# Splitting the tail of a decoder block into five stages, with the second token tile's layers ahead of the last two and the first expert dot products inside the first tile's queries

## The chip, the cores and the metric

The kernel runs on one core of a Trainium2 chip. The metric is the device time of one execution in microseconds; three runs of the kernel before gave 4187.27, 4188.42 and 4192.22 us, median 4188.42 us. Everything is in 32-bit floats.

## What is computed

One decoder block on 512 tokens of 2048 channels: a normalised and modulated input, a mixer (12 heads of windowed attention beside a convolution module, merged by two sigmoid gates and projected), a residual, a second norm, and a retrieval layer over 16384 single-neuron experts. Cut to what the change touches:

```python
y = (g_attn * attn + g_conv * conv) @ w_out        # "mix", then "out"
x = x + gate1 * rms_norm(y, g[1])
h = rms_norm(x, g[2]) * (1.0 + scale2) + shift2
q = (h @ w_q).reshape(B, S, 8, 2, 128)             # queries
s1, s2 = q[..., 0, :] @ sub_keys[:, 0], q[..., 1, :] @ sub_keys[:, 1]
v1, i1 = top_k(s1, 16); v2, i2 = top_k(s2, 16)
top, ci = top_k(v1[:, None] + v2[None, :], 16)     # 16 experts of each of 8 heads
gate = softmax(top)
pre = einsum('td,tkd->tk', h, expert_down[idx])    # 128 rows of 2048 for every token
out = einsum('tk,tkd->td', gelu(pre) * gate, expert_up[idx])
x = x + gate2 * rms_norm(out, g[3])
```

## The kernel before, in words

Each engine runs its own program and they meet at semaphores. The first part (to about 843 us) makes the projections, the attention and the convolution of all 512 tokens. What follows has two interleaved strands.

**The tail.** `TAIL` (L31) has two parts: tokens 0 to 127, then tokens 128 to 511. Each goes through the same steps, and each reads the weights again in chunks of 1 MB that SP loads into a ring of buffers (`T_KB`, L144: five buffers for the first part, three for the second; `put`, L489). One part is 48 chunks of the mix (four column groups `cg`, each of gate chunks `ga` x4, `gc` x4, attention projection `ao` x2 of half size, convolution projection `co` x2), 16 chunks of the output projection (`out`), one chunk of x per 128 tokens (`x`), and 16 chunks of the queries (`q`, four groups, each followed by the key scores `sc`). A chunk is 16 matmuls on TensorE of as many columns as the part has tokens. ScalarE applies the sigmoids and copies, VectorE the products, the norms, and then `route` (L1552, six steps that pick 16 experts for each of two heads) and `gates` (L1589, the end of the softmax, behind an exponential that ScalarE makes in `gate_exp`, L1127). POOL first loads 32 MB of modulation weights (L570 to L575, ring `ada_ring` of four), which VectorE sums in `condition` (L1516) while the first part's mix runs.

**The retrieval.** It goes in blocks: block b stands for 32 tokens times 4 of their 128 experts, so 512 blocks (`BLOCKS`), 128 for each tile of 128 tokens. POOL gathers 1 MB of expert rows for each block from the down table (L594) and, 22 blocks behind (`UP_LAG`), 1 MB from the up table (L602). Both gathers of one step of the loop stand in one queue, and each first waits until its buffer is free: a down buffer by VectorE's `dot` (L1602), an up buffer by TensorE's `weighted_rows` (L840), which runs 24 blocks behind (`LAG`). ScalarE makes the gelu and the block's weights (`unit_gelu`, `block_weights`); VectorE multiplies by the gates in `unit_act` once in 16 blocks. Once in 32 blocks TensorE turns the next rows of h (`h2_quarter`, with a copy by ScalarE after each quarter), and the 32 finished tokens are normalised and stored (`z_sum`, `x2_rows`, `finish`, `stores`).

**Their interleaving.** Each engine keeps a position in blocks, and `retrieve(upto)` brings it forward. In the second part of the tail each engine calls it after a chunk, or after some chunks (`chunk_out`, `passed`), with a block number from `PACE` (L121 to L126): block 128 at chunk 83, evenly. In the first part nothing of the retrieval runs. After the tail, `retrieve(END)` does the rest, 384 blocks. The gathers have three down and three up buffers up to block `WIDE` = 160, and five and five from there, some of which are the tail's memory, hence the waits at L592 and L600. SP loads the keys again for the second part once `routed` is 4 (L535).

## Time and profile before

| | us |
|---|---|
| median of three runs | 4188.42 |
| the profiled execution, device time | 4186.43 |
| its span, first to last instruction | 4184.6 |
| TensorE busy in the span | 2812.4 (67%) |
| VectorE busy | 2284.2 (55%) |
| POOL busy | 1391.0 (33%) |
| ScalarE busy | 541.4 (13%) |
| bytes moved by DMA | 1413.23 MB, 338 GB/s over the span |

The span is 1.8 us shorter than the device time of the same execution. The shares of busy time are averages over stages with different limits, so the stages have to be read one by one: the first tile's tail runs from 843 to 1151 us, the second part's from 1156 to 2164 us, and the retrieval alone from there to the end.

### The profile page before, as it was taken

Reading aid. Unit: us, or ns where it says so; the run is one execution under the profiler, and the core shown is the slowest. Engines: PE = TensorE matmul, PEld = TensorE weight load, DVE = VectorE, ACT = ScalarE, POOL = GpSimd, SP = SyncE. Lnnn points to the kernel's source line nnn. Section 1 sums busy time; section 2 is a strip of 40 time slices with the busy share of each in tenths; the row PEclk is TensorE's granted clock in tenths of the full one; section 3 lists DMA queues with packets and bytes.
Section 4 is the critical chain, followed back from the end, with each engine's and each line's share of the span. In section 5 each row is a group of like instructions: output and inputs, shape, how many; then the busy total and the mean of one; then the engine's idle time right before and its main releaser. Section 6 shows DMA issues by size and latency. Waiting matters only on the chain.

```text
span 4184.6 us, 37663 instructions
## 1 busy us (share of the span) xinstructions
PE 2812.4 (67%) x15140; PEld 1597.2 (38%) x15140; DVE 2284.2 (55%) x3525; ACT 541.4 (13%) x1191; POOL 1391.0 (33%) x1109
## 2 busy tenths in 40 slices
PE   5899899889899999997983434434444444434435
PEld 3687788789855555553540100100101101101101
DVE  6399779742564333325674665664666664444442
ACT  2221221200210101012120100100100110000000
POOL 2421211000012333322334454434434444344342
PEclk8899999999999999998985555555555555555556
DMA  9463434798658998986879999999999999999998
GB/s 350 145 217 130 156 100 142 278 370 318 211 207 322 370 375 344 378 330 244 336 288 421 393 405 421 421 422 421 421 421 417 422 421 415 421 422 419 422 421 369
DMA packets 303725, 1413.23 MB, mean 338 GB/s; under 512 B 24384, under 2 KB 24512, under 8 KB 167104
## 3 DMA queue, kind: packets, MB, share of 16 engines
q0 software_dynamic: 152064, 1107.36, 64.4%
q1 hardware_dynamic: 145568, 291.53, 19.7%
q10 hardware_dynamic: 5920, 11.94, 0.8%
q8 instruction: 120, 1.97, 0.2%
q14 instruction: 53, 0.43, 0.0%
HBM read 1403.35 MB, written 7.39 MB: 337 GB/s over the span
## 4 chain that ended last, share of the span: by engine, by line
PE 41%; DMA 38%; DVE 13%; POOL 3%; issue 3%; ACT 2%; SPq 0%; DVEq 0%; ACTq 0%; POOLq 0%
PE psum L608 41%; DMA front<-in_down,back 30%; DMA front<-in_up,back 5%; DVE front L1607 4%; POOL front L579 3%; DVE back L1375 2%; DMA front<-in_w_in 2%; DMA back<-in_ada_w 1%; DVE back L1344 1%; ACT back L1137 1%; POOL x_low L563 0%; DVE back L1708 0%; ACT front L1241 0%; DVE back L1442 0%; DVE w_low L1330 0%
## 5 line engine op out<-in xcount | busy, mean ns | idle before, releaser
L608 PE MATMUL psum<-front 128*32 128x512 f32 (+2 forms) x6608 | 1401.8, 662 | 934.5 <-DMA front<-in_up,back 851.6
L1607 DVE CUSTOM_DVE_ANT_0 front<-front,back 128x2048 f32<-128x2048 f32 x512 | 1171.2, 2292 | 1357.3 <-DMA front<-in_down,back 1230.0
L608 PEld LDWEIGHTS psum<-front 128*32 128x32 f32 (+1 forms) x6608 | 573.5, 161 | 1697.6 <-issue 1430.1
L579 POOL DMA_INDIRECT front<-in_down,back x512 | 596.9, 1166 | 913.8 <-DVE back L1607 666.6
L579 POOL DMA_INDIRECT front<-in_up,back x442 | 515.4, 1166 | 1003.3 <-PE psum L608 951.7
L608 PE MATMUL psum<-back,front 128*32 128x128 f32 (+3 forms) x4400 | 631.5, 453 | 312.7 <-DMA back<-in_up,back 174.5
L608 PEld LDWEIGHTS psum<-back,front 128*32 128x32 f32 (+1 forms) x4400 | 368.4, 166 | 582.1 <-issue 328.2
L557 POOL TENSOR_TENSOR w_low<-front,w_high 128x2048 fp32r<-128x2048 f32 x33 | 156.0, 4728 | 551.2 <-ACT w_high L1025 551.2
L608 PE MATMUL psum<-x_high,w_high 128*128 128x512 f32 x640 | 253.2, 396 | 7.8 <-POOL x_low L563 4.7
L608 PE MATMUL psum<-x_high,w_low 128*128 128x512 f32 x640 | 251.2, 393 | 0.0
L608 PE MATMUL psum<-x_low,w_high 128*128 128x512 f32 x640 | 251.1, 392 | 0.0
L608 PE MATMUL psum<-back 128*32 128x128 f32 (+5 forms) x1400 | 183.0, 393 | 61.4 <-DMA back<-in_ada_w 32.5
L1149 ACT ACTIVATE front<-back 128x32 f32<-128x32 f32 x512 | 116.2, 309 | 734.9 <-DVE back L1616 734.9
L608 PEld LDWEIGHTS psum<-back 128*128 128x128 f32 (+1 forms) x1400 | 135.2, 185 | 144.0 <-issue 78.7
L1344 DVE SCALAR_TENSOR_TENSOR back<-back 128x512 f32<-128x512 f32 x232 | 160.3, 767 | 0.0
L1025 ACT ACTIVATE w_high<-front 128x2048 fp32r<-128x2048 f32 x52 | 99.6, 1915 | 468.5 <-PE psum L608 409.5
L1375 DVE SCALAR_TENSOR_TENSOR back<-back 128x512 f32<-128x512 f32 x120 | 145.5, 1212 | 10.1 <-DMA back<-in_ada_w 4.6
L608 PEld LDWEIGHTS psum<-x_high,w_high 128*128 128x128 f32 x640 | 121.7, 190 | 35.4 <-POOL x_low L563 5.7
L608 PEld LDWEIGHTS psum<-x_low,w_high 128*128 128x128 f32 x640 | 121.8, 190 | 24.9
L608 PEld LDWEIGHTS psum<-x_high,w_low 128*128 128x128 f32 x640 | 121.4, 190 | 25.9
L1137 ACT ACTIVATE back<-psum 128x512 f32<-128x512 f32 x64 | 38.2, 597 | 576.2 <-DVE back L1607 407.1
L579 POOL DMA_INDIRECT back<-in_up,back x70 | 80.0, 1143 | 91.6 <-PE psum L608 87.1
(161 smaller groups left out, 1686.0 us busy)
## 6 DMA issues: line engine op xcount, KB each, us to landing
front<-in_w_in SPq DMA_DIRECT2D x116, 1024.0 KB, 7.4
back<-in_ada_w SPq DMA_DIRECT2D x64, 1024.0 KB, 9.0
front<-in_ada_w POOLq DMA_DIRECT2D x32, 1024.0 KB, 9.5
front<-in_w_out SPq DMA_DIRECT2D x32, 1024.0 KB, 6.3
front<-in_w_q SPq DMA_DIRECT2D x32, 1024.0 KB, 5.3
front<-in_w_conv_o SPq DMA_DIRECT2D x16, 1024.0 KB, 7.5
front<-in_w_attn_o SPq DMA_DIRECT2D x16, 512.0 KB, 9.3
front<-in_down,back POOLq DMA_INDIRECT x512, 17.2
```

Source lines behind the costliest of these rows:

```text
L557: nc.gpsimd.tensor_tensor(wl[s], ring[s], wh[s % 2].bitcast(fp32), ALU.subtract).then_inc(w_low_done, 1)
L579: nc.gpsimd.indirect_dma_start(out=row_, out_offset=None, in_=table[:, :], in_offset=bass.IndirectOffsetOnAxis(ap=idx4[:, t % 2, c:c + 1], ...
L608: return nc.tensor.matmul(o, a, b, start=start, stop=stop)
L1025: A(wh[s % 2], ring[s], ACT.Copy).then_inc(w_high_done, 1)
L1137: A(h2r[:, i * NT:(i + 1) * NT], ps[:, 7, :], ACT.Copy).then_inc(h2r_ready, 1)
L1149: A(diag[:, b % 32, :], same[:, 0:32], ACT.Copy, scale=actv[:, n % 2, b % 16:b % 16 + 1]).then_inc(diag_ready, 1)
L1344: last[c] = st.did(V.scalar_tensor_tensor(total, src, tap, total, ALU.mult, ALU.add))
L1375: ins = V.scalar_tensor_tensor(total, part, weight, total, ALU.mult, ALU.add)
L1607: V.tensor_tensor_reduce(d_row[s], d_row[s], h2r, 1.0, 0.0, ALU.mult, ALU.add, pre[:, b // 16 % 2, b % 16:b % 16 + 1]).then_inc(dots_done, 1)
```

## The change

The tail gets five stages: the mix of tile 0, the rest (out, x, queries) of tile 0, the mix of tiles 1 to 3 together, the rest of tile 1 alone, and the rest of tiles 2 and 3. `w_out` and `w_q` are so read three times instead of twice. The pace table reaches block 200 at the end of the tail instead of 128, and its first 16 blocks fall into the queries of tile 0 (third and fourth query group). The routing of tile 2 moves from `retrieve` into the last stage. The gates of tile 0 are all made behind its fourth routing, their exponentials too; `g3_rows` and its copy go ahead of the queries; in the stages of the rest the scores stand ahead of the last chunk's blocks, and the blocks that belong to the x chunks behind the second norm's squares. To make room for the early blocks, tail buffer 3 moves from 24 KB to 88 KB, where it has to wait for `h_joined` = 4, and the ring of modulation weights has three buffers instead of four. Tile 3's scores take the memory of tile 1's, and the down gathers get a fourth buffer there from block 128 and a sixth from `WIDE` = 208.

```diff
-TAIL = ((0, P), (P, S - P))
+STAGES = (("mix", 0, P), ("rest", 0, P), ("mix", P, S - P), ("rest", P, P), ("rest", 2 * P, S - 2 * P))
+FIRST = 1
...
-WIDE = 160
+WIDE = 208
...
+def tail_groups(c):
+    stage, t0, n = STAGES[c]
+    if stage == "mix":
+        return [(kind, cg, k) for cg in range(4) for kind, k in (("ga", 4), ("gc", 4), ("ao", 2), ("co", 2))]
+    return ([("out", i, 4) for i in range(4)] + [("x", t, 1) for t in range(n // P)]
+            + [(kind, i, k) for i in range(4) for kind, k in (("q", 4), ("sc", 0))])
...
 def tail_chunks(c):
-    return 4 * 12 + 16 + TAIL[c][1] // P + 16
+    return sum(k for _, _, k in tail_groups(c))
+
+ALONE = sum(tail_chunks(c) for c in range(FIRST))
+DEEP = sum(tail_chunks(c) for c in range(2))
...
-    return [(i + 1) * 128 // tail_chunks(1) for i in range(tail_chunks(1))]
+    out = [0] * 25 + [8] * 4 + [16] * 4
+    out += [16 + (i + 1) * 84 // 48 for i in range(48)] + [101 + i for i in range(16)] + [118]
+    out += [120, 123, 126, 128] + [128 + 8 * min(i, 2) for i in (1, 2, 3) for _ in range(4)]
+    out += [144 + 3 * (i + 1) // 2 for i in range(16)] + [172, 176]
+    out += [176 + 3 * (i + 1) // 2 for i in range(16)]
+    assert len(out) == len(ENDS) - ALONE
+    return out
+
+def reached(chunks):
+    return PACE[chunks - 1 - ALONE] if chunks > ALONE else 0
...
-D_KB, U_KB = (64, 72, 80, 0, 8), (88, 96, 104, 16, 169)
-D_SLOT = slot_table(BLOCKS, WIDE, 3, len(D_KB))
-U_SLOT = slot_table(BLOCKS, WIDE, 3, len(U_KB))
-T_KB = (0, 8, 16, 24, 96)
-T_SLOT = slot_table(tail_chunks(0) + tail_chunks(1), tail_chunks(0), len(T_KB), 3)
+D_KB, U_KB = (64, 72, 80, 160, 0, 8), (88, 96, 104, 16, 169)
+D_SLOT = slot_table(BLOCKS, (0, 3), (128, 4), (WIDE, len(D_KB)))
+U_SLOT = slot_table(BLOCKS, (0, 3), (WIDE, len(U_KB)))
+T_KB = (0, 8, 16, 88, 96)
+T_SLOT = slot_table(len(ENDS), (0, len(T_KB)), (DEEP, 3))
...
-        ada_ring = [view(64 + 8 * s, D) for s in range(4)]
+        ada_ring = [view(64 + 8 * s, D) for s in range(3)]
-        sc = [view(kb, KT, P) for kb in (169, 144, 152, 160)]
+        sc = [view(kb, KT, P) for kb in (169, 144, 152, 144)]
...
                 s, _, prev = T_SLOT[at]
+                if at == 3:
+                    sp.wait_ge(h_joined, 4)
...
-                if c == 1:
+                    if NTH[c] == 1:
                     sp.wait_ge(routed, 4)
                     nc.sync.dma_start(keys[1]...)
...
 # TensorE, rest(c)
-                    chunk_out(c)
+                    chunk_at += 1
                 for kk in range(8):
...
                     ins.then_inc(sqs_used if kk < 7 else ss_done, 1)
-                pe.wait_ge(h2_ready, KT * (c + 1))
+                retrieve(reached(chunk_at))
+                if r == 0:
+                    g3_rows()
+                pe.wait_ge(h2_ready, KT * (r + 1))
...
 # ScalarE, rest(c)
-                    passed(c, 1)
-                    if i:
-                        gate_exp(c, i - 1)
+                    passed(1)
+                    if r and i:
+                        gate_exp(r, i - 1)
+                for i in (range(3, 4) if r else range(4)):
+                    gate_exp(r, i)
...
 # VectorE, rest(c)
+                passed(n // P)
                 dve.wait_ge(std2_ready, 2 * r + 2)
...
                 for i in range(4):
-                    passed(c, 4)
+                    passed(4)
                     dve.wait_ge(act_took, ATOOK[c, "sc", i] + 4)
                     for step in range(6):
-                        route(c, i, step)
-                    if i:
-                        gates(c, i - 1)
-                gates(c, 3)
+                        route(r, i, step)
+                    if r and i:
+                        gates(r, i - 1)
+                for i in (range(3, 4) if r else range(4)):
+                    gates(r, i)
...
 # retrieve, VectorE and ScalarE
-                    if 2 <= t < TT and b % 128 >= 28 and n < 4:
+                    if t == TT - 1 and b % 128 >= 28 and n < 4:
```

## Rows read from the trace of the kernel before

**Rows 1.** The page: GB/s in 40 slices of 104.6 us.

```profile
GB/s 350 145 217 130 156 100 142 278 370 318 211 207 322 370 375 344 378 330 244 336 288 421 393 405 421 421 422 421 421 421 417 422 421 415 421 422 419 422 421 369
```

**Rows 2.** Windows: stretch, busy PE, PEld, DVE, ACT, POOL (instructions), clock, DMA share, GB/s.

```profile
1158.00:1264.00 106.00, 103.85 (x434) 61.63 (x433) 65.99 (x179) 11.68 (x17) 21.12 (x14) 0.99 0.58 217
1264.00:1689.00 425.00, 417.46 (x1790) 223.02 (x1788) 154.34 (x167) 40.80 (x108) 138.90 (x109) 1.00 0.91 353
1689.00:1958.00 269.00, 235.55 (x1019) 126.87 (x1019) 108.51 (x130) 43.15 (x90) 81.25 (x62) 0.94 0.86 330
1958.00:2164.30 206.30, 206.30 (x842) 113.63 (x842) 110.30 (x307) 29.92 (x101) 60.75 (x49) 0.99 0.80 304
2164.30:4184.60 2020.30, 840.43 (x5243) 189.74 (x5242) 1082.52 (x1680) 187.22 (x567) 887.46 (x789) 0.54 0.99 412
```

**Rows 3.** DMA queues, 1264 to 1689 us: packets, MB, share of 16 engines.

```profile
q0 software_dynamic: 15522, 113.01, 66.5%
q1 hardware_dynamic: 18333, 36.96, 24.2%
```

**Rows 4.** TensorE in time: chunk of 384 columns, blocks, chunks of 128 columns, a turned quarter.

```profile
1397.53 1.92 PE L608 MATMUL psum<-front 128*32 128x512 f32 x16
...
1399.39 10.59 PE L608 MATMUL psum<-back,front 128*128 128x384 f32 x32
...
1022.44 14.46 PE L608 MATMUL psum<-back,front 128*128 128x128 f32 x128
...
1169.81 1.08 PE L608 MATMUL psum<-back,front 128*32 128x128 f32 x32 [0.72 <-ACT back L1137]
```

**Rows 5.** Timeline at the tail's start: VectorE's joins, TensorE's squares, the wait behind.

```profile
783.12 6.68 DVE L1458 TENSOR_TENSOR front<-x_high,x_low 128x2048 f32<-128x2048 f32 x3
...
792.41 7.03 PE L608 MATMUL psum<-back 128*128 128x512 f32 x16
...
799.55 0.69 DVE L1479 TENSOR_SCALAR back<-psum 128x512 f32<-128x512 f32 x1 [7.47 <-PE psum L608]
```

**Rows 6.** Windows, columns as rows 2: DMA after the joins.

```profile
790.00:810.00 20.00, 20.00 (x136) 16.17 (x135) 11.32 (x26) 14.61 (x24) 2.33 (x4) 1.00 1.03 404
843.00:1000.00 157.00, 136.62 (x1120) 135.29 (x1119) 67.25 (x65) 7.25 (x25) 12.15 (x22) 0.91 0.99 374
```

**Rows 7.** VectorE in time: two routings, gates and what follows, dot products 1 and 13.

```profile
1106.17 0.88 DVE L1530 MAX8 back<-back 128x8 f32<-128x128 f32 x4 [21.88 <-ACT back L1252]
...
1124.03 0.88 DVE L1530 MAX8 back<-back 128x8 f32<-128x128 f32 x4
...
1162.92 0.19 DVE L1593 TENSOR_REDUCE back<-back 128x2 f32<-128x32 f32 x1
...
1166.11 0.87 DVE L1530 MAX8 back<-back 128x8 f32<-128x128 f32 x4
...
1210.93 2.29 DVE L1607 CUSTOM_DVE_ANT_0 front<-front,back 128x2048 f32<-128x2048 f32 x1
...
1252.26 2.29 DVE L1607 CUSTOM_DVE_ANT_0 front<-front,back 128x2048 f32<-128x2048 f32 x1 [0.47 <-DMA front<-in_down,back]
```

**Rows 8.** TensorE: tile 0's last out chunks, first queries, last scores.

```profile
1052.81 10.88 PE L608 MATMUL psum<-back,front 128*128 128x128 f32 x96
...
1088.84 16.09 PE L608 MATMUL psum<-front 128*128 128x128 f32 x128 [8.47 <-ACT front L1241]
...
1150.40 1.06 PE L608 MATMUL psum<-front,back 128*128 128x128 f32 x8
```

**Rows 9.** DMA issues from 2164.3 us to the end.

```profile
front<-in_down,back POOLq DMA_INDIRECT x383, 22.2
front<-in_up,back POOLq DMA_INDIRECT x336, 22.5
...
back<-in_up,back POOLq DMA_INDIRECT x70, 22.5
```

More of the change, by code:

```diff
@@ L949, in tail, with rest, squares @@
                         modulation_columns(2)
+            def rest(c):
+                nonlocal chunk_at
+                (_, t0, n), r = STAGES[c], NTH[c]
+                def squares(buf, count, first, last):
+                    for i in range(count):
+                        ins = mm(ps[:, 6, 0:n], ones, buf[:, i, 0:n], first and i == 0, last and i == count - 1)
+                    return ins
                 for i in range(4):
@@ L985, in tail @@
                     else:
-                        group(4, 4, hT, plain, act_took, ATOOK[c, "sc", i - 1])
-                    for m in range(4):
-                        pe.wait_ge(act_took, ATOOK[c, "q", i] + m + 1)
-                        for t in range(n // P):
-                            ins = mm(ps[:, m, t * P:(t + 1) * P], sqt[:, m, t * P:(t + 1) * P], keys[c][:, 4 * i + m, :], True, True)
-                        ins.then_inc(g_done, 1)
-            tail(0)
-            g3_rows()
-            tail(1)
+                        group(4, 4, hT, plain, t0, n, act_took, ATOOK[c, "sc", i - 1], None, scores)
@@ L996, in _ @@
+            for c, (kind, _, _) in enumerate(STAGES):
+                if kind == "mix":
+                    mix(c)
+                else:
+                    rest(c)
             retrieve(END)
```

302 lines of the change are left out of this document (157 added, 145 removed).

## The prediction

> **What bounds the kernel now.** I read the page's slices first. From about 2200 us to the end the traffic stands at 421 GB/s in nearly every slice [rows 1]. A gather of 1 MB (1.0486 MB) at that rate takes 2.49 us, and nothing but gathers is left there, so this stage is bound by the DMA engines, and its length is the number of gathers left when the tail ends. Next the windows by stage [rows 2]: in the tail of tiles 1 to 3 TensorE is busy 98% of 1264 to 1689 us at full clock while the DMA share is 0.91; from 1689 to 1958 the share is 0.86, from 1958 to 2164 it is 0.80, and in the first column group (1158 to 1264) only 0.58. So before 2164 us TensorE sets the pace and leaves DMA time over; after it, DMA does. A change wins if it puts gathers into that spare time, and each gather so placed gives back 2.49 us.
>
> The spare time is limited. Weighted by length, the shares leave 45 + 38 + 38 + 41 = 162 us idle between 1158 and 2164 us. The queues' rows give the price of work in the mixed stage [rows 3]: q0 moved 107.8 gathers in 66.5% of 425 us, 2.6 us each; q1 35.2 chunks in 24.2%, 2.9 us each.
>
> **Part by part.**
>
> *More weights.* 16 chunks of `w_out` and 16 of `w_q` more, 32 x 2.9 = 93 us of DMA time. This stands against the 162 us above before anything else is counted.
>
> *The moved tail buffer.* The fourth chunk now waits for the joins of h, which end at 789.8 us [rows 5]. TensorE used it before 792.4 and then made the squares for which VectorE waits at 799.55 [rows 5]. The chunk now lands some 7 to 12 us after 789.8, with the modulation loads issued at the same moment, and the DMA engines are full from 790 us on (404 GB/s; 0.99 from 843 to 1000) [rows 6], so the loads held back on SP's queue, this chunk and those behind it, fall into a full stage. I take +10 us (bounds 5 and 18). The modulation ring of three costs nothing: the stage is bound by the sum of the bytes, and VectorE's long wait for TensorE in each column group covers a later load. Without that cover it would be one load, 3 us, in a group.
>
> *The first tile's queries.* Nothing changes until the second group's scores. Routing takes 17.9 us a group (1106.17 to 1124.03), gates 3.2 us, and 13 dot products with three buffers took 43.6 us, 3.35 each [rows 7]. VectorE now does route, route, 8 dots, route, 8 dots, route, four gates: from 1106.2 it is 35.7 + 26.8 + 17.9 + 26.8 = 1213.4 when the fourth routing starts, 1231 at its end, 1244 behind the gates. TensorE ended the scores at 1151.5 [rows 8]; the four quarters of h2, 1.8 us each [rows 4], come forward into them: 1159. It makes the next stage's first gate chunks to 1200. Then it stalls: ScalarE stands at the fourth exponential, which comes some 11 us into the fourth routing, 1224, so its sigmoids come at 1228 (28 us of wait). Two chunks on, at 1249, TensorE wants the first block's weights, which need six more dots behind 1244: 1264 (15 us). The rest of the group is 2 chunks of 10.3 us [rows 4], two half ones and two more whole ones for 31, the next quarters of h for 7, and 12 blocks of `weighted_rows` at 0.93 [rows 4], so it ends at 1334, with the +10 at 1344. Before it ended at 1264. By then 37 blocks are dotted instead of 18.
>
> *Column groups 2 to 4.* A group has 11 chunks' worth of bytes and now 21 blocks: DMA 11 x 2.9 + 42 x 2.6 = 141 us; TensorE 11 x 10.3 + 21 x 0.93 and some 6 for quarters and norms = 139. Before it was 134 by the same sum and took 425 / 3 = 141.7 [rows 2]. Two resources equally full: I take 145 (bounds 140 and 155). The mix ends at 1779, with blocks at 100; before, at 1689 with 74.
>
> *Rest of tile 1.* 33 chunks, the keys, 44 blocks. DMA 34 x 2.9 + 88 x 2.6 = 328 us. TensorE: 3.6 us a chunk (14.46 for four) [rows 4], 119 + 41 + quarters, 175. So DMA bounds it. The norm between out and queries takes 25 us at 128 columns (1063.7 to 1088.8) [rows 8], about what nine free buffers absorb. The gathers of blocks 128 and 136 wait for a routing that VectorE only begins after its dots: twice some 8 us. I take 345; it ends at 2124.
>
> *Rest of tiles 2 and 3.* 34 chunks, 56 blocks: 34 x 2.9 + 112 x 2.6 = 390 us of DMA against 34 x 6.9 + 52 = 290 of TensorE and 128 + 84 of VectorE. The norm, with two tiles of x and twice the columns, lies between tile 0's 25 us and twice that [rows 8]. I take 405; the tail ends at 2529 instead of 2164.
>
> *What is left.* Before, 383 down and 406 up gathers were issued behind 2164 [rows 9] and the stage took 2020.3 us [rows 2]. Now 72 fewer of each: 144 x 2.49 = 359 us less, 1662. The sixth down buffer brings nothing to a stage that is at 421 GB/s.
>
> **The sum**: 2529 + 1662 = 4191 us of span, 4192.5 with what lies around it, 6 above the profiled execution's 4186.4. That one stood 2 us under the median of 4188.4, so the forecast is 4194. In short: 365 us more tail for 359 us less of the rest.
>
> **The rivals.**
>
> *A, faster: the tail runs at the DMA engines' own rate.* With 9 or 10 buffers always in flight, groups 2 to 4 take 140 each, the rest 330 and 392. For it: the mix of tile 0 ran at share 0.99 with nine buffers [rows 6]. Against: no row shows 0.99 for three queues of work with routing between. It gives 15 + 15 + 13 = 43 less, 4151; with gathers at 2.49 instead of 2.6 up to 25 less again.
>
> *B, slower: the engines wait for one another in the short stages.* POOL's queue is in order, so a down gather stands behind an up gather that waits for TensorE, TensorE waits for ScalarE, and ScalarE for a dot product. In the two rests VectorE makes eight routings of 17.9 us in one piece, and during each the down buffers fill and POOL stops. For it: shares of 0.86 and 0.80 in these very stages before [rows 2], though TensorE was full. If the rests come to 0.90 instead of the 0.96 I take, they last 798 instead of 750: 4242. It decides from the share at which they take over 757 us.
>
> *C, slower: TensorE's clock.* In the last stage, busy 42%, it was granted 0.54 of full speed, that is mostly 1.2 GHz [rows 2]. In the rest of tile 1 it is wanted for 175 of 345 us in bursts between loads. At half speed a chunk and a block need 7.2 + 1.9 = 9.1 us against 8.1 of DMA, so TensorE bounds the stage: 33 chunks make +25 to +30 us, 4221. It decides from a granted clock under about 0.57. In the other rest TensorE would be busy throughout at half speed, and a busy TensorE had full clock in every such row. The Trainium skill ("TensorE: Matmul & The Clock Gate", HAM oscillation) says that matmul bursts shorter than the DMA waits between them leave the clock throttled in each burst. By that rule C comes true in the rest of tile 1; the last stage's 0.54 agrees, while the mix of tile 0, also of 128 columns and waiting for DMA, had 0.91 [rows 6].
>
> *D: the early dots bring nothing.* They take VectorE's time before the routing is over, and TensorE waits 43 us for it. If blocks had started only in the mix, its first group would end some 45 us earlier with 16 fewer blocks, 80 us of gathers. So they pay, unless the stall is twice what I reckon: 4235.
>
> **How the numbers follow.** Forecast 0.38, with its own range 4175 to 4215; A 0.30; B 0.20; C 0.09; D 0.03. A measurement of this kernel can tell some 0.2%, 8 us, from no change, so faster is below 4180, slower above 4197. Faster: all of A and 0.07 of the forecast, 0.37. Within: 0.20, the forecast's middle. Slower: 0.11 of the forecast and B, C, D, 0.43. The range takes A's 4151 with some of its second step at the lower end, and B at the upper: 4138 to 4248.
>
> **What would show it.** The last stage begins near 2529 us with 421 GB/s in nearly every slice; the page shows 1447 MB moved. TensorE idles about 28 and 15 us between 1200 and 1275 us, for ScalarE's sigmoids and for block weights. VectorE's wait at L1479's line ends near 810. The first stage's end shifts by about 10 us. The two rests together take 750 us at a share near 0.96, the clock in the first over 0.6. The forecast is wrong if they take under 715 or over 790, if the mix's groups differ from 145 by over 8, or if the last stage is not 359 us shorter.

## The result, and the profile after

The changed kernel takes 4232.30 us (median of five runs, 4221.79 to 4240.16) against 4188.42 us before (five runs, 4181.12 to 4197.02): a ratio of 1.0105, interval 1.0088 to 1.0122, so it is slower by 44 us, about 1%. The forecast was 4194. The result lies inside the range of 4138 to 4248, but outside the forecast's own 4175 to 4215, close to rival B's 4242. The profiled execution took 4232.28 us with a span of 4230.5, 45.9 us more than the span before, and this is the difference that the stages below have to add up to.

The page of the changed kernel, clock, DMA share and GB/s in 40 slices of 105.8 us:

```profile
PEclk8999999899988999987689696555555555555555
DMA  9463433798669999999799798999999999999999
GB/s 357 143 226 113 159 121 109 263 386 325 223 245 372 379 370 409 397 406 381 278 367 408 284 381 358 389 407 421 421 422 421 421 421 419 421 421 421 421 421 373
DMA packets 320631, 1446.94 MB, mean 342 GB/s; under 512 B 24896, under 2 KB 25024, under 8 KB 184000
```

The slices at 421 GB/s now begin with the 28th; before, the first was the 22nd, with two lower ones behind it [rows 1]. The bytes are the 1447 MB foretold. The windows by stage of the changed kernel, columns as in [rows 2]:

```profile
1164.00:1355.00 191.00, 135.06 (x554) 73.62 (x553) 116.52 (x286) 16.64 (x42) 61.51 (x44) 0.83 0.77 298
1355.00:1790.00 435.00, 424.36 (x1899) 221.53 (x1898) 165.96 (x174) 47.31 (x117) 167.79 (x127) 1.00 0.98 389
1790.00:1946.00 156.00, 105.69 (x759) 85.00 (x757) 59.72 (x74) 22.01 (x77) 46.62 (x40) 0.85 0.99 394
1946.00:2160.00 214.00, 121.42 (x919) 85.05 (x920) 113.62 (x285) 21.58 (x78) 61.73 (x49) 0.70 0.83 327
2160.00:2404.00 244.00, 179.44 (x1022) 124.78 (x1020) 126.88 (x254) 39.11 (x102) 88.70 (x67) 0.86 0.93 371
2404.00:2566.00 162.00, 149.35 (x896) 113.08 (x897) 102.77 (x303) 25.11 (x73) 58.57 (x43) 0.97 0.89 353
2566.00:4230.50 1664.50, 700.34 (x4250) 157.62 (x4248) 841.41 (x1162) 150.37 (x469) 951.81 (x649) 0.53 0.99 412
```

The lines are the first column group, the other three, tile 1's out and norm, its queries, tiles 2 and 3's out and norm, their queries, and the retrieval alone. Two things stand out. The mix runs at a DMA share of 0.98 with TensorE busy 98%: that part of the plan works. And tile 1's queries run at 0.83 with TensorE busy 57% and VectorE 53%: nothing is full there.

**A ledger of lost time.** A share mixes rows of 2 and of 8 KB, so I count differently: a stage of length L at a rate of R GB/s could have moved its bytes in L x R / 421, and the rest, L x (1 - R / 421), is lost. Before, the four windows of the tail in [rows 2] lose 51 + 69 + 58 + 57 = 235 us. Here the first six lose 56 + 33 + 10 + 48 + 29 + 26 = 202. So the change recovers 33 us in the tail, and 8 more in the last stage (36 lost instead of 43, which is 356 us shorter). But it moves 33.7 MB more, 80 us at 421 GB/s, and the tail starts 5 us later, below. 80 - 33 - 8 + 5 = 44, of 45.9 measured; the rest is the rounding of the rates to 1 GB/s. **The change buys 41 us of lost time with 80 us of weights.**

The stages, forecast against measured ends in us of the span:

| | forecast | measured | added to the miss |
|---|---|---|---|
| start of tile 1 to 3's mix, late by | 10 | 5 | -5 |
| first column group ends | 1344 | 1361 | +22 |
| mix ends | 1779 | 1794 | -2 |
| tile 1's rest ends | 2124 | 2160 | +21 |
| tail ends | 2529 | 2566 | +1 |
| last instruction | 4191 | 4230.5 | +2.5 |

One trace is one execution: in the runs below that have the same program up to the mix's end (e4, e5, e6, e8) TensorE starts the next stage at 1787, 1798, 1790 and 1794 us, here at 1795. A difference of a few us in one stage of one trace is therefore not read as an effect.

**The start.** In time, TensorE's loads and squares at the tail's start and VectorE's wait for them; [rows 5] had this last line at 799.55:

```profile
778.19 10.88 PE L638 MATMUL psum<-front 128*128 128x128 f32 x96
794.96 5.95 PE L638 MATMUL psum<-front 128*128 128x128 f32 x32 [5.89 <-DMA front<-in_w_in]
...
807.89 0.69 DVE L1527 TENSOR_SCALAR back<-psum 128x512 f32<-128x512 f32 x1 [15.75 <-PE psum L638]
```

TensorE waits 5.9 us for the chunk that was held back for the joins, and VectorE goes on 8.3 us later. By the end of the first tile's out chunks 5.3 us of it are left (1066.39 instead of 1061.05).

**The first column group.** TensorE and ScalarE in time:

```profile
1172.20 44.54 PE L638 MATMUL psum<-front 128*128 128x384 f32 x128 [7.74 <-issue]
1232.39 0.23 ACT L1173 ACTIVATE back<-back 128x32 f32<-128x32 f32 x1 [46.83 <-DVE back L1618]
1236.10 22.68 PE L638 MATMUL psum<-front 128*128 128x384 f32 x64 [19.36 <-ACT back L1243]
1275.17 1.93 PE L638 MATMUL psum<-front 128*32 128x512 f32 x8 [16.39 <-DMA front<-in_up,back]
...
1320.37 1.06 PE L638 MATMUL psum<-back,front 128*32 128x128 f32 x32
1329.42 1.94 PE L638 MATMUL psum<-back,front 128*32 128x128 f32 x32 [8.00 <-ACT back L1180]
```

This is the stall as foretold: four gate chunks, then nothing until ScalarE, which stood at the fourth exponential (1232.39), makes the sigmoids; two chunks more; then the wait for the first block. The forecast had TensorE going on at 1238 and 1274 with the late start in it; it did at 1236.1 and 1275.2, behind waits of 19.4 and 16.4 us for 28 and 15. What it had too short is what comes after: 86 us instead of 70. The turned quarters took 16 us instead of 7, with an 8 us wait for ScalarE's copy and 1.94 us each instead of 1.08 [rows 4], at a granted clock of 0.65 from 1320 to 1337 us; the blocks took 14 us instead of 11 and another 3 us wait (at 1280), and the chunks 54 instead of 52.

**Tile 1's rest.** TensorE in time, in the out chunks (first two lines) and the queries:

```profile
1809.85 5.42 PE L638 MATMUL psum<-back,front 128*128 128x128 f32 x32 [5.09 <-DMA front<-in_w_out]
1821.50 6.37 PE L638 MATMUL psum<-back,front 128*128 128x128 f32 x32 [5.24 <-DMA front<-in_w_out]
...
2035.65 1.94 PE L638 MATMUL psum<-front 128*32 128x512 f32 x8 [16.69 <-DMA front<-in_up,back]
...
2103.43 1.93 PE L638 MATMUL psum<-front 128*32 128x512 f32 x8 [22.12 <-DMA front<-in_up,back]
```

The waits of the stage, 1790 to 2160 us (who, for whom: us in total, times, longest):

```profile
POOL front L609 <- PE psum L638: 133.8, 32, 15.1
PE psum L638 <- DMA front<-in_up,back: 86.2, 18, 22.1
POOL front L609 <- DVE back L1633: 64.9, 2, 35.6
```

These three lines are a circle. At blocks 128 and 136 POOL stands at a down gather whose indices VectorE has yet to choose (65 us in two waits). The up gathers behind it in POOL's queue are not waiting for anything of their own, but are not issued; so TensorE stands 16.7 and 22.1 us at a block; and it hands no buffer back, so that POOL, once free, waits for TensorE.

Of TensorE's clock: 0.85 and 0.70 of full speed were granted in the two halves of tile 1's rest. The 16 out chunks, 32 matmuls each, took 72.3 us together. The six that came behind a wait of 3.1 to 6.0 us for their load took 5.4 to 6.4 us each, the other ten 3.84. The Trainium skill ("TensorE: Matmul & The Clock Gate", HAM oscillation) tells of DMA waits longer than the matmul bursts between them, after each of which the next burst starts throttled. Throttled throughout, a chunk would take an estimated 7.2 us, twice the 3.6 of [rows 4]; the trace agrees in that the six were slowed, but for a part of their time only, and the measurement decides.

### The profile page after: what moved, and what is told of

Its sections match the earlier page's. It is cut to its first block, busy times and chain, and to the rows that moved or that the text cites. A ratio compares the mean times of both kernels' runs of the same rounds, so it can differ in the third digit from the quotient of the medians.

```text
span 4230.5 us, 39946 instructions
## 1 busy us (share of the span) xinstructions
PE 2826.2 (67%) x16228; PEld 1743.8 (41%) x16228; DVE 2285.0 (54%) x3535; ACT 551.0 (13%) x1262; POOL 1646.1 (39%) x1109
## 4 chain that ended last, share of the span: by engine, by line
DMA 43%; PE 34%; DVE 14%; POOL 5%; issue 3%; ACT 2%; SPq 0%; DVEq 0%; ACTq 0%; POOLq 0%
PE psum L638 34%; DMA front<-in_up,back 22%; DMA front<-in_down,back 7%; DMA back<-in_up,back 4%; POOL front L609 4%; DMA front<-in_w_out 3%; DMA back<-in_down,back 2%; DVE back L1423 2%; DMA front<-in_w_in 2%; DVE front L1655 2%; DMA back<-in_ada_w 1%; DVE back L1392 1%; DMA front<-in_w_q 1%; DVE back L1633 1%; ACT back L1180 1%
## 5 line engine op out<-in xcount | busy, mean ns | idle before, releaser
L638 PE MATMUL psum<-front 128*32 128x512 f32 (+3 forms) x7200 | 1412.6, 617 | 960.8 <-DMA front<-in_up,back 826.6
L1655 DVE CUSTOM_DVE_ANT_0 front<-front,back 128x2048 f32<-128x2048 f32 x441 | 1008.6, 2292 | 1276.1 <-DMA front<-in_down,back 1158.2
L638 PEld LDWEIGHTS psum<-front 128*128 128x128 f32 (+1 forms) x7200 | 645.6, 164 | 1652.1 <-issue 1381.0
L609 POOL DMA_INDIRECT front<-in_down,back x441 | 739.7, 1677 | 555.3 <-DVE back L1633 252.5
L609 POOL DMA_INDIRECT front<-in_up,back x452 | 517.8, 1146 | 1100.5 <-PE psum L638 1060.1
L638 PE MATMUL psum<-back,front 128*32 128x128 f32 (+4 forms) x4832 | 636.0, 420 | 308.1 <-DMA back<-in_up,back 148.4
L638 PEld LDWEIGHTS psum<-back,front 128*32 128x32 f32 (+1 forms) x4832 | 435.1, 172 | 531.4 <-issue 288.9
L1655 DVE CUSTOM_DVE_ANT_0 back<-back 128x2048 f32<-128x2048 f32 x71 | 162.7, 2291 | 165.2 <-DMA back<-in_down,back 165.0
L638 PEld LDWEIGHTS psum<-back 128*128 128x128 f32 (+1 forms) x1464 | 145.6, 186 | 136.6 <-issue 72.6
L609 POOL DMA_INDIRECT back<-in_down,back x71 | 122.9, 1731 | 21.9 <-issue 21.9
```

The costliest lines, as they stand in the source:

```text
L609: nc.gpsimd.indirect_dma_start(out=row_, out_offset=None, in_=table[:, :], in_offset=bass.IndirectOffsetOnAxis(ap=idx4[:, t % 2, c:c + 1], ...
L638: return nc.tensor.matmul(o, a, b, start=start, stop=stop)
L1655: V.tensor_tensor_reduce(d_row[s], d_row[s], h2r, 1.0, 0.0, ALU.mult, ALU.add, pre[:, b // 16 % 2, b % 16:b % 16 + 1]).then_inc(dots_done, 1)
```

## The experiments

The medians and ratios to the kernel before, which ran beside each of them on the same chip. Two rows of the table differ clearly only from about 0.0024 on, 10 us, since each has an interval of its own:

| run | what it is | median us | ratio | interval |
|---|---|---|---|---|
| (the change) | | 4232.30 | 1.0105 | 1.0088 to 1.0122 |
| e1_slot | before, buffer moved | 4194.75 | 1.0015 | 1.0006 to 1.0025 |
| e2_early | before, early blocks too | 4238.97 | 1.0121 | 1.0104 to 1.0138 |
| e3_split | the split alone | 4228.16 | 1.0091 | 1.0075 to 1.0108 |
| e4_quarter | last two tiles' rest, a quarter of its weight bytes | 4215.64 | 1.0071 | 1.0054 to 1.0088 |
| e5_late | blocks 128 to 144 behind tile 1's queries | 4226.48 | 1.0083 | 1.0066 to 1.0099 |
| e6_norm | no blocks in the last two norms | 4241.20 | 1.0128 | 1.0111 to 1.0145 |
| e7_all | e3 with e5's and e6's pace | 4235.70 | 1.0107 | 1.0090 to 1.0124 |
| e8_quarter1 | tile 1's rest, a quarter of its weight bytes | 4199.01 | 1.0017 | 1.0007 to 1.0027 |
| e9_share | w_out read twice | 4184.16 | 0.9991 | 0.9981 to 1.0001 |
| e10_share8 | e9, blocks 128 to 144 in tile 1's queries | 4213.26 | 1.0057 | 1.0040 to 1.0074 |
| e11_held | e9, six to twelve blocks held back | 4200.34 | 1.0029 | 1.0017 to 1.0042 |
| e12_held | e9, up to sixteen blocks held back | 4200.10 | 1.0026 | 1.0014 to 1.0037 |

### The parts one by one

**e1_slot**: the kernel before with the moved buffer and the shorter modulation ring.

```diff
-T_KB = (0, 8, 16, 24, 96)
+T_KB = (0, 8, 16, 88, 96)
+                if at == 3:
+                    sp.wait_ge(h_joined, 4)
-        ada_ring = [view(64 + 8 * s, D) for s in range(4)]
+        ada_ring = [view(64 + 8 * s, D) for s in range(3)]
```

> The kernel before with only the moved tail buffer and the modulation ring of three. The trace of after has tile 0's last out copies 5.3 us later than before. Theory (bytes against idle time, the start shifted by 5): 5 us slower, 4193, and the shift is seen already at the first norm of tile 0. Rival (the held-back loads find room later, since TensorE waits elsewhere anyway): within 2 us of before.

Measured: 6 us slower. VectorE's wait at the tail's start ends as in the changed kernel, timeline:

```profile
807.62 0.69 DVE L1481 TENSOR_SCALAR back<-psum 128x512 f32<-128x512 f32 x1 [15.70 <-PE psum L610]
```

So 6 us of the 44 are the buffer's and the ring's together (2 to 10 by the interval). The term of 10 was a little high, inside its bounds.

**e2_early**: the early 16 blocks with the softmaxes behind the routings, the moved buffer, and tiles 1 to 3 in one part as before; the tail ends at block 128 and gathers widen at 160.

```diff
-    return [(i + 1) * 128 // tail_chunks(1) for i in range(tail_chunks(1))]
+    out = [0] * 25 + [8] * 4 + [16] * 4
+    out += [16 + (i + 1) * 112 // 83 for i in range(83)]
+    return out
```

> The first 16 blocks in tile 0's queries, its softmaxes behind them and the moved buffer, but tiles 1 to 3 stay one part of 384 columns and the tail ends at block 128 as before. Theory: the tail of this kernel is bound by TensorE, so the two waits of the first column group (28 and 15 us in the forecast, 1200 to 1275 us) and the 5 us of the start all come out at the end: 35 to 45 us slower than before, about 4228, with no word of DMA. Rival (the early gathers pay): 16 gathers of 2.49 us less behind the tail, 4150 to 4190.

Measured: 50 us slower, somewhat more than the 35 to 45 of the theory. Of the 50, 6 are the moved buffer's (e1) and 44 the early blocks' with their softmaxes. Windows, columns as above: the tail behind tile 0, its second half (1689 to 2213 us), and what is left.

```profile
1164.00:2213.00 1049.00, 966.20 (x3968) 524.06 (x3970) 443.83 (x851) 124.54 (x324) 284.60 (x226) 0.97 0.81 308
1689.00:2213.00 524.00, 477.80 (x1978) 261.48 (x1980) 220.99 (x448) 77.83 (x207) 129.37 (x106) 0.96 0.78 293
2213.00:4233.80 2020.80, 850.33 (x5250) 192.89 (x5242) 1081.81 (x1677) 186.12 (x561) 886.54 (x791) 0.53 1.00 413
```

The tail ends 49 us later and nothing is earned, since its length is TensorE's work plus the stall and its number of blocks is the same as before. 16 blocks that came early only leave the later chunks with fewer to gather (293 GB/s from 1689 on, where [rows 2] had 330 and 304).

**e3_split**: the changed kernel without what the early blocks brought: no block before tile 1's mix, tail buffers, modulation ring and softmaxes as before. The six down buffers stay.

```diff
-    out = [0] * 25 + [8] * 4 + [16] * 4
-    out += [16 + (i + 1) * 84 // 48 for i in range(48)] + [101 + i for i in range(16)] + [118]
+    out = [0] * 33
+    out += [(i + 1) * 100 // 48 for i in range(48)] + [101 + i for i in range(16)] + [118]
```

> The second tile's layers alone, three readings of w_out and w_q, block 200 at the tail's end, but no blocks in tile 0's queries, buffers and softmaxes as before; the mix of tiles 1 to 3 takes blocks 0 to 100. Theory (DMA bound from the mix on): removing the waits of the first group buys little, because the 16 gathers have to be made up in a mix that has no DMA time to spare; 0 to 15 us under the changed kernel, 4217 to 4232. Rival (the stall of the first group is the loss): 40 us under it, 4190.

Measured: 4228.16, 4 us under the changed kernel, which is within the spread of the two. Windows of the first column group and the other three:

```profile
1164.00:1355.00 191.00, 162.66 (x680) 92.15 (x683) 101.03 (x184) 19.24 (x40) 60.11 (x42) 0.93 0.78 300
1355.00:1783.00 428.00, 390.39 (x1850) 201.41 (x1851) 166.38 (x169) 48.55 (x118) 170.33 (x130) 0.95 0.98 393
```

By 1355 us it has moved as much as the changed kernel (300 against 298 GB/s) with half of TensorE's idle time (28 us instead of 56, 20 of it one wait for VectorE), and the other groups are held by DMA (0.98) with TensorE at 91%. The early blocks cost 44 us where TensorE is the bound and nothing clear of the spread where it is the bytes. The split alone already carries the loss, and neither part is worth anything alone.

### Where the split loses

**e4_quarter** and **e8_quarter1** take the bytes away in one stage each: `w_out` and `w_q` chunks of 128 rows instead of 512 (for e8 with `c == 3`). The other three quarters of each chunk are then what the buffer held, so the tokens of that stage come out wrong.

```diff
-                            rows(w_out, s * NT, NT, i * NT)
+                            rows(w_out, s * NT, NT, i * NT, c == LAST)
-                            rows(w_q, s * NT, NT, i * NT)
+                            rows(w_q, s * NT, NT, i * NT, c == LAST)
```

> The changed kernel, but in the last stage each load of w_out and w_q brings a quarter of its bytes (the other three quarters of the chunk are what the buffer held, so the last 256 tokens are computed with wrong weights). 32 loads lose 24 MB. Theory (the stage is bound by bytes): 24 x 2.9 = 70 us of DMA less, 50 to 70 us faster than the changed kernel, 4162 to 4182, under the kernel before. Rival (the engines wait for one another in the short stages, whatever the bytes): under 20 us faster, above 4212.

Measured: 4215.64, only 17 us under the changed kernel for 25 MB less, 60 us at 421 GB/s: the rival's range, not the theory's. The last two tiles' rest, by windows:

```profile
2154.00:2545.00 391.00, 327.66 (x1933) 238.77 (x1932) 231.84 (x560) 65.13 (x179) 150.11 (x111) 0.91 0.82 319
```

It still takes 391 us instead of 406, now at a share of 0.82. What holds it is shown by the changed kernel's windows inside this stage: out chunks and norm; the queries' line stands in the table above.

```profile
2160.00:2316.00 156.00, 145.41 (x861) 107.74 (x860) 77.88 (x187) 20.56 (x57) 62.32 (x47) 0.98 1.00 399
2316.00:2404.00 88.00, 34.03 (x162) 17.05 (x161) 49.00 (x68) 18.55 (x45) 26.38 (x20) 0.65 0.79 321
```

TensorE is busy 93% and 92% of out chunks and queries, and between them lies a norm of 88 us in which it works 34. ScalarE alone waits 36.7 us there for VectorE's `L1768`, the products of the second norm, which stand behind eight dot products. So this stage has two bounds close together: the bytes, 0.91 of 406 us or some 370, and TensorE's chunks with the norm between them, 145 + 88 + 149 = 382. That they don't keep in step all the time, hence 406, is a reading of these shares; with the bytes cut, the chain is left, at 391.

> The changed kernel, but the weight loads of the rest of tile 1 bring a quarter of their bytes (tile 1 is computed with wrong weights). 24 MB less, in the stage in which TensorE waited for loads of w_out at a granted clock of 0.85 and 0.70. Theory (this stage, not the last, is the one bound by bytes): its out chunks lose 12 x 2.9 = 35 us, its queries less than 10; 35 to 45 us faster than the changed kernel, about 4192, where the same cut in the last stage gave 17. Rival (TensorE's low clock bounds the stage): under 15 us faster, as a chunk takes as long as before.

Measured: 4199.01, 33 us under the changed kernel, just short of the theory's 35 to 45 and far from the rival's range, under 15. It is still 1.0017 times the kernel before: with three quarters of the second tile's weight bytes gone, the split is not ahead either. Windows of tile 1's out and norm, and its queries:

```profile
1783.00:1915.00 132.00, 101.06 (x778) 78.05 (x776) 62.38 (x78) 18.89 (x68) 45.09 (x43) 0.94 0.91 367
1915.00:2128.00 213.00, 120.38 (x917) 83.04 (x918) 113.02 (x282) 24.64 (x86) 62.98 (x50) 0.70 0.72 286
```

Out and norm go from 156 to 132 us (151 to 125 between TensorE's first out chunk and its first query chunk), and the queries stay at 213 us with half of the stage's byte cut in them: they are not bound by bytes at all. The first half is bound by bytes, the second by engines that wait for one another, the circle of three waits. In the first half the granted clock rose with the cut, from 0.85 to 0.94, so the lower clock there came with the waits for loads. In the queries it was 0.70 in both runs, so this run says nothing of what the clock costs there.

**e5_late**, **e6_norm**, **e7_all** move blocks out of the places where they make a queue wait, by the pace alone. e5 takes blocks 128 to 144 out of tile 1's queries, where they wait for a routing:

```diff
-    out += [120, 123, 126, 128] + [128 + 8 * min(i, 2) for i in (1, 2, 3) for _ in range(4)]
-    out += [144 + 3 * (i + 1) // 2 for i in range(16)] + [172, 176]
+    out += [120, 123, 126, 128] + [128] * 12
+    out += [128 + 5 * (i + 1) // 2 for i in range(16)] + [172, 176]
```

> The changed kernel with another pace table alone: blocks 128 to 144 no longer fall into the query groups of tile 1 but into the next stage's out chunks (2.5 blocks a chunk instead of 1.5). In after, TensorE waits there 16.7 and 22.1 us for up gathers that stand in POOL's queue behind a down gather that waits for a routing, and the DMA share of 1946 to 2160 us is 0.83. Theory (two limits close together, TensorE's chain and the bytes): both waits vanish, the queries take some 100 us instead of 214, and the next out chunks are bound by DMA at 254 us instead of 156; 10 to 20 us faster than the changed kernel, 4212 to 4222. Rival (in-order waits between the engines are the whole loss): 35 us or more faster, under 4197.

Measured: 4226.48, 6 us under the changed kernel, which is within the spread of the two. Windows of tile 1's queries, and the next out chunks:

```profile
1946.00:2064.00 118.00, 87.02 (x661) 75.32 (x662) 73.21 (x246) 18.79 (x68) 22.60 (x22) 0.83 0.90 349
2064.00:2316.00 252.00, 185.55 (x1137) 123.33 (x1135) 117.74 (x226) 27.66 (x83) 110.97 (x76) 0.86 0.91 368
```

The queries are 96 us shorter, and the out chunks behind them, now with the 16 blocks more, also 96 longer. TensorE's work in the queries is 34 us less (87 instead of 121), so 62 of the 96 were not work of TensorE: the circle is real. But the gathers it held up have to be made somewhere. The out chunks had a DMA share of 1.00 in the changed kernel and could not take them in; now they run at 0.91 with TensorE busy 74%, and the time comes back.

e6 ends both norms' blocks ahead of the norm:

```diff
-    out += [16 + (i + 1) * 84 // 48 for i in range(48)] + [101 + i for i in range(16)] + [118]
+    out += [16 + (i + 1) * 84 // 48 for i in range(48)] + [101 + i for i in range(16)] + [116]
...
-    out += [144 + 3 * (i + 1) // 2 for i in range(16)] + [172, 176]
-    out += [176 + 3 * (i + 1) // 2 for i in range(16)]
+    out += [144 + 3 * (i + 1) // 2 for i in range(16)] + [168, 168]
+    out += [168 + 2 * (i + 1) for i in range(16)]
```

> The changed kernel with another pace table alone: no blocks within the norms of the last two stages (2 and 8 before); they go into the queries behind. With a quarter of the weight bytes the last stage got only 17 us shorter, and ScalarE waits 37 us there for VectorE's second norm, which stands behind eight dot products. Theory (the chain of the engines and the bytes are both near the limit): the wait of 37 us vanishes, and the queries become DMA bound with 32 blocks instead of 24, about 204 instead of 162 us; within 10 us of the changed kernel. Rival (the chain alone bounds the last stage): 25 to 37 us faster, 4195 to 4207.

Measured: 4241.20, 9 us over the changed kernel, within the spread of the two and of the theory's 10. TensorE's first query chunk of the last stage, in the changed kernel and here; its last out chunk had ended at 2318.1 and 2322.2 us:

```profile
2405.33 20.09 PE L638 MATMUL psum<-front 128*128 128x256 f32 x89 [18.70 <-ACT front L1285]
...
2372.78 29.12 PE L638 MATMUL psum<-front 128*128 128x256 f32 x136 [11.62 <-ACT front L1285]
```

Windows of the norm and of the queries here:

```profile
2322.00:2373.00 51.00, 19.15 (x91) 13.27 (x90) 30.96 (x53) 16.60 (x33) 3.75 (x4) 0.76 0.54 216
2373.00:2570.00 197.00, 170.85 (x986) 122.55 (x986) 119.80 (x316) 29.94 (x93) 82.55 (x60) 0.92 0.93 372
```

The norm lasts 51 us instead of 87, and ScalarE's wait for `L1768` falls from 36.7 to 3.1 us. So eight blocks inside the norm cost it 36 us. But the queries, with those blocks more, take 197 us instead of 162, close to the 204 of the theory, and the tail ends where it did. Both mechanisms of the theory are seen, and they cancel.

> The split of the second tile alone (no early blocks, buffers and softmaxes as before), with both new paces: no blocks behind the routings of tile 1 and none within the norms. Theory (gains of the single steps add, the floor is the bytes): 4 of e3_split, 15 and 5, so about 4208, still slower than the kernel before, because 93 us of weight reading are bought with at most 150 us of idle DMA time of which some always stays. Rival (the engines' waits are the loss): under 4180, faster than before.

Measured: 4235.70, a miss by 28 us. The measured ratios of the three parts, each against the change's 1.0105, add up to 1.0105 - 0.0014 - 0.0022 + 0.0023 = 1.0092, which its interval still holds: each of the three is within the spread by itself, so the sum says only that nothing large was missed. Whether any of them survives in it is open.

### Half the extra weights

**e9_share** keeps the out chunks and the norm of tiles 1 to 3 together and splits the queries alone, so `w_q` is read three times and `w_out` twice. No early blocks; tail buffers and modulation ring as before, the six down buffers as in the change; the tail ends at block 156, and tiles 2 and 3 are routed within the retrieval. So it is not the change less 16 chunks alone: it also brings 44 blocks fewer forward.

```diff
-STAGES = (("mix", 0, P), ("rest", 0, P), ("mix", P, S - P), ("rest", P, P), ("rest", 2 * P, S - 2 * P))
+STAGES = (("mix", 0, P), ("out", 0, P), ("ask", 0, P), ("mix", P, S - P), ("out", P, S - P), ("ask", P, P), ("ask", 2 * P, S - 2 * P))
...
+    out = [0] * 33 + [(i + 1) * 100 // 48 for i in range(48)] + [100 + 3 * (i + 1) // 2 for i in range(16)] + [124, 125, 126] + [127, 128] + [128] * 14 + [128 + 28 * (i + 1) // 16 for i in range(16)]
```

> A version that reads half as much again: the output projection, x and both norms of tiles 1 to 3 stay together in 384 columns, and only the queries are split, tile 1 alone and tiles 2 and 3 behind it, so w_out is read twice and w_q three times (16 MB more than before, not 32). No early blocks, buffers and softmaxes as before; block 100 at the end of the mix, 128 before the queries, 156 at the tail's end, tiles 2 and 3 routed within the retrieval as before. Theory (bytes against idle time): 16 loads x 2.9 = 46 us of DMA less than in the changed kernel and no stage of 128 columns that waits for w_out, so some 45 us faster than it: 4180 to 4195, level with the kernel before. Rival (the split of the queries itself costs, by the routing between): above 4205.

Measured: 4184.16, ratio 0.9991 with 1 in its interval: level with the kernel before, 48 us under the change. Windows of the tail behind tile 0, of 110 us that start with tile 1's queries, and of what is left:

```profile
1158.00:2303.00 1145.00, 1021.09 (x4892) 602.04 (x4891) 518.95 (x943) 137.97 (x358) 376.12 (x286) 0.94 0.88 345
2050.00:2160.00 110.00, 92.69 (x781) 83.40 (x781) 86.62 (x374) 13.76 (x43) 9.76 (x9) 0.90 0.68 239
2303.00:4182.20 1879.20, 792.30 (x4944) 184.77 (x4943) 1001.15 (x1518) 178.09 (x539) 1099.47 (x736) 0.54 1.00 415
```

**e10_share8**: blocks 128 to 144 inside tile 1's queries, into the idle time that the second line shows.

```diff
-[127, 128] + [128] * 14 + [128 + 28 * (i + 1) // 16 for i in range(16)]
+[126, 127, 127, 128] + [136] * 4 + [144] * 8 + [144 + 12 * (i + 1) // 16 for i in range(16)]
```

> e9_share with blocks 128 to 144 inside tile 1's queries, eight behind each of the first two routings, as the changed kernel has them; block 156 at the end as there. Theory (two limits close together): within 8 us of e9_share, either sign, as e5_late was to the changed kernel. Rival (gathers behind a routing stall TensorE for nothing): 15 us or more slower than e9_share.

Measured: 4213.26, 29 us over e9: the rival's case. Windows of its tail, of the same 110 us, and of the stage behind tile 1's queries:

```profile
1158.00:2330.00 1172.00, 1012.97 (x4838) 589.42 (x4837) 526.41 (x948) 141.16 (x362) 363.69 (x284) 0.92 0.87 340
2050.00:2160.00 110.00, 59.48 (x528) 43.34 (x528) 57.57 (x185) 13.08 (x41) 25.75 (x22) 0.73 0.69 262
2219.00:2330.00 111.00, 111.00 (x563) 90.08 (x562) 53.72 (x167) 15.91 (x54) 23.58 (x21) 1.00 0.90 331
```

The block for which TensorE stands longest, timeline:

```profile
2163.60 1.94 PE L634 MATMUL psum<-front 128*32 128x512 f32 x8 [21.82 <-DMA front<-in_up,back]
```

In these 110 us the DMA share rises by 0.01 and TensorE's work falls from 93 to 59 us. Tile 1's queries, from TensorE's first chunk to the next stage's first, take 169 us instead of 73. The stage behind them has 16 blocks fewer left and is shorter, 111 us for 183, but there TensorE is busy without a pause, so it gives back only 72 of the 96. In the changed kernel undoing the circle gave 6 us, in the spread (e5), where the stage behind it had its DMA share at 1.00. That this difference in the stage behind makes 29 us of one and 6 of the other is argued from the shares, not tried by itself.

**e11_held** and **e12_held** hold back 6 and 14 blocks in the mix, 12 and 16 by the end of the out chunks, and give them to tile 1's queries, still ahead of block 128.

```diff
-[(i + 1) * 100 // 48 for i in range(48)] + [100 + 3 * (i + 1) // 2 for i in range(16)] + [124, 125, 126] + [127, 128] + [128] * 14
+[(i + 1) * 94 // 48 for i in range(48)] + [94 + 18 * (i + 1) // 16 for i in range(16)] + [114, 116, 118] + [118 + 10 * (i + 1) // 12 for i in range(12)] + [128] * 4
```

> e9_share with another pace table alone. Its trace leaves the DMA engines idle from 2000 to 2150 us (shares 0.46, 0.86, 0.45), in the norm and the queries of tile 1, while the mix before ran at 0.97 to 0.99. Blocks of tile 0 need no further routing, so some are held back for that stretch: 94 at the mix's end instead of 100, 112 instead of 124 behind the out chunks, 6 in the norms, 10 over tile 1's queries, then 128 to 156 as before. Theory (the time is bytes plus idle DMA time, wherever it lies): some 60 us of idle there, of which up to half is filled, 15 to 30 us faster than e9_share, 4155 to 4170, faster than both kernels. Rival (the norm and the queries are a chain of engines, and blocks in them only make it longer): within 5 us of e9_share or slower.

Measured: 4200.34, 16 us over e9, a miss: the rival's case. Windows of the tail, and of 150 us of the out chunks, where e9 had a share of 0.91 and TensorE also busy all 150:

```profile
1158.00:2321.00 1163.00, 1021.16 (x4893) 602.43 (x4892) 519.80 (x944) 140.46 (x359) 373.39 (x286) 0.93 0.87 341
1800.00:1950.00 150.00, 150.00 (x524) 80.59 (x523) 30.00 (x27) 16.28 (x44) 31.22 (x26) 1.00 0.75 279
```

> As e11_held, with more held back: 86 at the mix's end, 108 behind the out chunks, 114 behind the norms, 14 blocks over tile 1's queries. Theory: the mix falls under its DMA limit and TensorE bounds it again, so the further gain is small, within 8 us of e11_held. Rival (the chain only gets longer): slower than e11_held by 10 us or more.

Measured: 4200.10, the same. TensorE's work in the tail is 1021 us in e9 and in e11, and e11's tail is 18 us longer, so it is TensorE that idles more. Its first chunk of tile 1's queries and of tiles 2 and 3's show where, in e9 (first two lines) and e11:

```profile
2046.41 19.06 PE L634 MATMUL psum<-front 128*128 128x128 f32 x144 [12.91 <-ACT front L1288]
2119.80 7.10 PE L634 MATMUL psum<-front 128*128 128x256 f32 x32
...
2034.19 18.79 PE L634 MATMUL psum<-front 128*128 128x128 f32 x144 [21.83 <-ACT front L1288]
2139.72 7.10 PE L634 MATMUL psum<-front 128*128 128x256 f32 x32
```

With fewer blocks between them the out chunks end 36 us earlier in e11 (1952 instead of 1988). Then the norm, with six blocks in it instead of two, takes 82 us instead of 58, and tile 1's queries, with ten instead of two, take 106 instead of 73, in which TensorE waits 22 us for loads of `w_q` instead of 6. That is 36 us won and 56 lost. The idle DMA time of norm and queries is filled in part (0.65 and 0.90, where e9 had 0.58 and 0.78), at the price of the chain of engines in them, as in e6.

### The ledger over all runs

Bytes as time at 421 GB/s, and lost time as above in the tail behind tile 0 and in the rest, each as a difference to the kernel before (235 and 43 us lost there):

| | bytes | lost in the tail | lost in the rest | sum | span, measured |
|---|---|---|---|---|---|
| the change | +80 | -33 | -8 | +39 | +45.9 |
| e2_early | 0 | +47 | -5 | +42 | +49.2 |
| e3_split | +80 | -28 | -8 | +44 | +46.9 |
| e9_share | +40 | -28 | -16 | -4 | -2.4 |
| e10_share8 | +40 | -10 | -3 | +27 | +31.6 |
| e11_held | +40 | -14 | -16 | +10 | +15.5 |

The first two also start some 5 us later, which the columns leave out; the rest, up to 5 us, is of the size that the rounding of the rates allows, about 1 us in each 1000 of every window. The ledger is bookkeeping and proves no cause, but it says which size a cause has to explain. Only e9 wins back what it reads more.

## Why the prediction was right or wrong

- **What bounds the kernel**: right. The retrieval alone fell by 355.8 us for 359 foretold, and cut bytes give time back where DMA is the bound (e8's first half) and little or none elsewhere (e4, e8's second half).
- **More weights, 93 us against 162 idle**: the price was a little high. 33.7 MB are 80 us by the ledger. A span 6 us over the one before with a start 10 late meant 93 + 4 = 97 us of idle time filled; at that same price 93 - 41 = 52 were.
- **The moved buffer, +10**: +5 to +6 (e1).
- **The first tile's queries and the stall**: TensorE went on within 2 us of the forecast's times, if behind a shorter first wait and from an earlier start. The step that failed is "the rest of the group", 70 us: it took 86, since quarters and blocks were priced from rows at full clock with nothing to wait for, and the group came out of a stall. Shown by the trace alone; what the 17 us cost in the end is little, by e3, which has half the idle time in that group and is only 4 us faster, in the spread, as its mix is held by the bytes. So D, that the early dots bring nothing, is close to true as well, though in another way than its 4235: they are not dear, but without them the time is the same.
- **Groups 2 to 4 at 145**: (1794 - 1361) / 3 = 144, right. The share was 0.98, and A's 140 did not come with it.
- **Rest of tile 1 at 345**: the step that failed most, 366. I gave the routing's hold "twice some 8 us"; it was 16.7 and 22.1 at TensorE and 65 at POOL. And I took DMA for the bound of the whole stage; it is of its first half only. This is near B, which named the in-order queue and the stage, but not B's own chain: B had POOL stopped by full down buffers, and that wait was 13.8 us; the 65 are for indices that VectorE had not yet chosen, the wait that the forecast itself counted and made too small.
- **Rest of tiles 2 and 3 at 405**: 406, the right number from half a reason. "390 us of DMA against 290 of TensorE" left the norm out of TensorE's side. I had it between 25 and 50 us, and it takes 51 by itself (e6), but 87 with the eight blocks that I put into it. With it TensorE's side is 382, and e4 shows that the bytes alone were not it. That 405 and 406 agree is luck.
- **The rivals**: A fell (no stage behind the mix holds 0.99 through). B came half true: the two rests took 772 us, over its threshold of 757 and under its 798, at its share of 0.90 and 0.91. Chunks and gathers cost about 2% less than I priced them, which is most of the difference. C fell by its own sign: the clock was 0.70 and above, over its 0.57, and TensorE was busy 68% and 57% of the two halves. No run takes the clock by itself, so what 0.85 and 0.70 cost is not measured. D, see above.

In all, of the 39.5 us of span missed, 15 came by the end of the mix, 21 in tile 1's rest and 3.5 behind it. The 15 are partly the spread of one trace (above). The sum put the price of the change about right and its yield too high: the queues were taken as full wherever the sums said that they could be.

## What to carry to other kernels

To read weights again so as to start a transfer-bound stage earlier pays only for idle transfer time that is really filled. Price the bytes at the full rate. Of the idle time count only the part in which no transfer stands, in an in-order queue, behind one that waits for an engine's result. When two resources are within some per cent of each other, moving work between stages moves the idle time at best (e5, e6) and adds waits at worst (e10, e11); of the splits tried here, only those with fewer bytes ended clearly earlier than the changed kernel (e4, e8, e9 and its variants). And a part that costs 44 us alone can cost nothing beside another, so parts are to be tried in the company they will keep.

## What the runs showed of the hardware that I had not expected

- Weight loads arrive much later when gathers fill the engines, at the same size. Median from issue to landing of `w_out`'s 1 MB: 7.1 us for the 13 that the kernel before issued behind 1689 us, at a share of 0.86, but 17.6 us in tile 1's rest. DMA issues there:

```profile
front<-in_w_out SPq DMA_DIRECT2D x17, 1024.0 KB, 17.6
```

With three buffers that is one load in 5.9 us, and TensorE waits 33.9 us for them in 9 waits, with the engines at 0.99. The loads of `w_q` in the same stage, most of them issued in its second half at 0.83, took 6.3 us. The Trainium skill ("DMA: Bandwidth & Descriptors", Issuing engines are not separate DMA queues) says that transfers started from different engines run on the same 16 DMA engines and interleave; the trace agrees, the loads of SP's queue were slower where POOL's gathers filled the engines. No run varies the gathers alone.

- A gather from the down table took POOL longer to issue in the changed kernel, 1677 ns, against 1146 for one from the up table (groups of the page):

```profile
L609 POOL DMA_INDIRECT front<-in_down,back x441 | 739.7, 1677 | 555.3 <-DVE back L1633 252.5
L609 POOL DMA_INDIRECT front<-in_up,back x452 | 517.8, 1146 | 1100.5 <-PE psum L638 1060.1
```

The mean of the down gathers is 1144 to 1166 ns in the three kernels with five down buffers (before, e1, e2) and 1.6 us or more in the others, with six. From 3000 to 3030 us the down gathers, each issued 0.3 us after an up gather, take 2.0 us, and the up gathers, which wait 1.7 us for their buffer first, 0.94. POOL is busy 57% of that stage and DMA has a share of 0.99 in it, so it is not the bound there; what makes it, and whether it costs anything elsewhere, was not tried.
